# Order of the expert units' buffers, an earlier split of the fourth expert unit, and float32 down units in every other expert

## The reference

```python
logits = jnp.einsum('btd,de->bte', x, router).astype(jnp.float32)
top_v, top_i = lax.top_k(logits, TOP_K)
top_w = jax.nn.softmax(top_v, axis=-1)
...
for e in range(N_EXPERTS):
    out = out + comb[..., e:e + 1] * swiglu(x, w_gu[e], w_dn[e])
```

## Time and profile before

| | us |
|---|---|
| median of 3 runs | 1188.5 |
| lowest, highest | 1188.1, 1192.33 |
| the profiled execution | 1189.18 |
| its span | 1187.5 |
| PE busy | 1131.7 (95% of the span) |
| DVE busy | 948.0 (80%) |
| ACT busy | 715.5 (60%) |
| expert stage, first gate matmul to last down matmul | 748.6 to 1135.4 |
| mean TensorE clock granted | 0.991 of full speed |

### The profile page before, as it was taken

How to read it: one execution, slowest core, us unless ns; L and a number is a source line. 1 busy time by engine, 2 the same in 40 slices (tenths; PEclk the granted TensorE clock), 3 DMA queues, 4 the chain that set the end, 5 groups by cost and what they waited for, 6 DMA issues and landing times.

```text
span 1187.5 us, 31256 instructions
## 1 busy us (share of the span) xinstructions
PE 1131.7 (95%) x13743; PEld 1003.3 (84%) x13743; DVE 948.0 (80%) x1026; ACT 715.5 (60%) x730; POOL 24.9 (2%) x59
## 2 busy tenths in 40 slices
PE   7999999999999999899999998889998999999997
PEld 4788888878888888688888885889998998989976
DVE  5986896777666658996788678689899889898976
ACT  4555644455555445446564435777978669688653
POOL 4000001000000001000000100000000000000000
PEclk8999999999999999999999999899999999999999
DMA  9665566546555654356566564699999999999901
GB/s 268 220 212 178 182 209 215 178 143 205 184 194 195 210 183 142 123 186 207 191 205 202 185 211 153 241 392 393 394 392 393 385 382 394 387 393 390 378 20 38
DMA packets 195673, 289.56 MB, mean 244 GB/s; under 512 B 5208, under 2 KB 132200, under 8 KB 195543
## 3 DMA queue, kind: packets, MB, share of 16 engines
q1 hardware_dynamic: 193830, 283.71, 68.4%
q0 software_dynamic: 1728, 4.16, 1.3%
HBM read 286.53 MB, written 1.52 MB: 243 GB/s over the span
## 4 chain that ended last, share of the span: by engine, by line
PE 82%; DVE 12%; issue 3%; ACT 3%; DMA 0%; SPq 0%; DVEq 0%; ACTq 0%
PE acc L595 16%; PE acc L597 16%; PE acc L596 16%; DVE wl L1361 6%; PE acc L909 4%; PE acc L874 4%; PE acc L877 4%; PE acc L876 4%; PE acc L580 2%; PE acc L581 2%; PE acc L587 2%; PE acc L929 2%; PE acc L926 2%; PE acc L928 2%; PE aux L827 2%
## 5 line engine op out<-in xcount | busy, mean ns | idle before, releaser
L1361 DVE SCALAR_TENSOR_TENSOR wl<-raw,wh 128x2048 f16<-128x2048 f32 x177 | 403.8, 2288 | 116.7 <-ACT wh L1007 116.3
L595 PE MATMUL acc<-xn,wh 128*128 128x264 f16 x1424 | 393.0, 276 | 2.2 <-DVE wl L1361 2.2
L597 PE MATMUL acc<-xn,wl 128*128 128x264 f16 x1424 | 393.0, 276 | 0.0
L596 PE MATMUL acc<-xn,wh 128*128 128x264 f16 x1424 | 393.0, 276 | 0.0
L1007 ACT ACTIVATE wh<-raw 128x2048 f16<-128x2048 f32 x177 | 336.0, 1908 | 1.4 <-PE acc L877 0.6
L874 PE MATMUL acc<-ga,wh 128*128 128x96 f16 x1536 | 204.5, 207 | 10.9 <-issue 5.7
L877 PE MATMUL acc<-ga,wl 128*128 128x96 f16 x1536 | 204.4, 207 | 5.6 <-issue 5.6
L876 PE MATMUL acc<-ga,wh 128*128 128x96 f16 x1536 | 204.3, 207 | 2.1 <-issue 2.1
L874 PEld LDWEIGHTS acc<-ga,wh 128*128 128x128 f16 x1536 | 151.5, 99 | 13.9 <-issue 12.3
L595 PEld LDWEIGHTS acc<-xn,wh 128*128 128x128 f16 x1424 | 139.3, 98 | 23.6 <-ACT wh L1007 2.5
L596 PEld LDWEIGHTS acc<-xn,wh 128*128 128x128 f16 x1424 | 139.3, 98 | 21.0
(11 more groups left out here) (307 smaller groups left out, 1934.1 us busy)
## 6 DMA issues: line engine op xcount, KB each, us to landing
raw<-in_w_in SPq DMA_DIRECT2D x56, 1024.0 KB, 5.1
raw<-in_moe_w_gu SPq DMA_DIRECT2D x42, 1024.0 KB, 13.4
raw<-in_ffn_w_gu SPq DMA_DIRECT2D x24, 1024.0 KB, 5.1
raw<-in_moe_w_dn SPq DMA_DIRECT2D x18, 1024.0 KB, 14.3
raw<-in_ffn_w_dn SPq DMA_DIRECT2D x12, 1024.0 KB, 5.1
ya<-in_moe_w_gu SPq DMA_DIRECT2D x11, 1024.0 KB, 13.6
ot_rows<-in_moe_w_gu SPq DMA_DIRECT2D x10, 1024.0 KB, 13.3
xa<-in_moe_w_gu SPq DMA_DIRECT2D x10, 1024.0 KB, 13.0
```

What stands on the lines that cost most here:

```text
L595: nc.tensor.matmul(bank, hi, x[:, 0, x0 + k, :], start=(k == 0), stop=False)
L596: nc.tensor.matmul(bank, hi, x[:, 1, x0 + k, :], start=False, stop=False)
L597: last = nc.tensor.matmul(bank, lo, x[:, 0, x0 + k, :], start=False, stop=(k == k_chunks - 1))
L1361: op(V.scalar_tensor_tensor(out=wl[:, s, 0:size], in0=raw_slot[raw_turn(n)[0]][:, 0:size], scalar=WS, in1=wh[:, s, 0:size], op0=ALU.mult, ...
```

## The change

Three things are changed. The order of the raw buffers is another: `raw` 2 moves back by two places and `raw` 3 by three, to the last of the ten, and OT, XB, XN, XA and UB come one place earlier each. The fourth expert unit is split in the routing stage: its `hi` stands behind that of the third, its `lo` behind the first one-hot. And only experts 0, 2, 4 and 6 keep direct units: the last two down units of experts 1, 3 and 5 are split like the others. `split_groups` counts the split groups up to q, for the waits.

```diff
-TURN_OF_SLOTS = (YA, 0, 1, 2, OT, XB, 3, XN, XA, UB)
+TURN_OF_SLOTS = (YA, 0, 1, OT, XB, 2, XN, XA, UB, 3)
...
-DIRECT = {dn_unit(e, d) for e in range(NE - 1) for d in range(MOE_DN - 2, MOE_DN)}
+DIRECT = {dn_unit(e, d) for e in range(0, NE, 2) for d in range(MOE_DN - 2, MOE_DN)}
...
-    return q % GROUPS < SPLIT_GROUPS or q // GROUPS == NE - 1
+    return q % GROUPS < SPLIT_GROUPS or q // GROUPS % 2 == 1
+
+
+def split_groups(q):
+
+    return sum(is_split(i) for i in range(q + 1))
...
-                    pe.wait_ge(hid_ready, 2 * FFN_IT + SPLIT_GROUPS * e + d // 2 + 1)
+                    pe.wait_ge(hid_ready, 2 * FFN_IT + split_groups(GROUPS * e + d // 2))
...
             hi(N_MOE + LEAD - 1)
+            hi(N_MOE + LEAD)
             norm_hi()
...
             def gate_or_up(e, u):
                 n, q = gu_unit(e, u), GROUPS * e + u // 4
-                hi(ahead(n))
+                if n > N_MOE:
+                    hi(ahead(n))
...
-                vec_e.wait_ge(hid_hi, q // GROUPS * SPLIT_GROUPS + q % GROUPS + 1)
+                vec_e.wait_ge(hid_hi, split_groups(q))
...
-                lo(ahead(n))
+                if n > N_MOE:
+                    lo(ahead(n))
...
             one_hot(0, sel_ready)
+            lo(N_MOE + LEAD)
             slot_weights(0)
```

More of the change, by code:

```diff
@@ L230, in program @@
         hid_32 = w1_half[:, n_split:4 * EC * CAP].bitcast(F32).rearrange("p (r n) -> p r n", r=2)
-        hid_last = w1_half[:, n_split:4 * EC * CAP].rearrange("p (r s n) -> p r s n", r=2, s=2)[:, (NE - 1) % 2]
+        hid_last = w1_half[:, n_split:4 * EC * CAP].rearrange("p (r s n) -> p r s n", r=2, s=2)[:, 1]
         def hid_half(q, i):
```

## The result

| | median | against before |
|---|---|---|
| before, 7 runs | 1188.65 us (1185.62 to 1192.33) | |
| changed, 7 runs | 1192.14 us (1191.26 to 1194.37) | ratio 1.0031, 95% interval 1.0016 to 1.0045, so +1.9 to +5.3 us |
| profiled execution of changed | 1193.02 us, span 1191.3 | before: 1189.18, span 1187.5 |

A forecast was written before the change was run, and what follows sets the result against it. The prediction took the loop ACT, DVE, PE to bound the expert stage, with DMA just keeping up. Delays of 1.1 + 1.1 + 0.8 = +3.0 us at three turn ends gave 1191.5 us, range 1183.5 to 1196.5.

The forecast's parts named there:

- Bound: Expert stage: bound by the loop ACT, DVE, PE, with PE last; the DMA queue keeps up and no more.
- Buffers and early split: Routing stage and first loads: earlier transfers and early split of the fourth unit, cost 0, gain 0.
- the 8.5 us of head start: Expert loads: four earlier transfers put loading 8.5 us ahead, worth nothing by itself as no engine waits for a transfer.
- The cost of PE beside a busy DMA: PE from 744 to 754 us: gaps of about 1 us could appear beside now busy DMA engines, 0 to +1.
- DVE's lag: Ends of turns 2, 4, 6: extra `lo` work delays the next turn's first down unit, +1.1, +1.1, +0.8 us.
- PE's saving: Turns 2, 4, 6: split units save PE 3.1 us each, 9.4 in all, which do not come out.
- Behind the boundary: After turn 2: PE leads again, DVE's lag shrinks from 1.6 to 0.6 us, under the slack; turns 4 and 5 repeat it.
- The sum: Whole kernel: 1.1 + 1.1 + 0.8 = +3.0 us, so 1191.5; bounds +1 to +5, chance 0.59.
- DMA wall: Rival, expert stage: bytes alone bound it, so loading 8.5 us earlier ends 8.5 us earlier, 1180.0; chance 0.12.
- Shorter gaps: Rival, turns 3 and 5: PE's gaps are fetches queued behind weight packets and halve, 4 us, giving 1187.5; chance 0.11.
- DVE not refilled: Rival, ends of turns 2, 4, 6: DVE still waits for ACT, 3.9 us each, 1200.2, half refilled 1196; chance 0.13.

The follow-up runs named there:

- e_small_loads: Kernel before, each expert unit moved by two transfers of half its size on the same queue: -0.2 us against before (-1.8 to +1.4).
- e_buffers: Changed kernel with the direct units of before, so only the new buffer order and early split: +1.0 us against before (-0.2 to +2.1).
- e_half_after: Changed kernel, only the first half of each expert unit's rows transferred from the 21st unit on, stale values otherwise: +1.1 us against before (-0.5 to +2.6).
- e_units: Changed kernel with the buffers and loads of before, so only the six more split down units: +3.7 us against before (+2.4 to +4.9).
- e_buffers_hold: Kernel before plus new buffer order and early split, transfer into XN held until the first gather ends on PE: -1.8 us against before (-2.7 to -0.7).
- e_half_loads: Kernel before, only the first half of each expert unit's rows transferred from the 21st unit on, stale values otherwise: -11.1 us against before (-12.8 to -9.4).
- e_hold: Changed kernel with the transfer into XN held until the first gather ends on PE: +1.0 us against before (-0.2 to +2.1).

## Why the prediction came out right, step by step

- **Bound.** That no engine waits for a transfer was right for the stretch that was read, 760 to 1060 us. Behind it ACT does, up to 3.2 us at 1107.8, and it costs nothing there; in e_small_loads even some 16 us of such waits cost nothing. Loading stands closer behind the loop than I had it. That PE is last in a loop of three was half of it: the loop alone would run 93.9 us a pair. I had seen the gaps of 1.02 and 0.95 us in the earlier trace rows and took them for a fixed price.
- **Buffers and early split.** Four issues, the DMA rate, the early `hi` and the early `lo` came where they were put, the issue into YA 3.3 us later (4.7 less the 1.4 by which the stage begins later), so the 8.5 us of head start were not reached. The cost of PE beside a busy DMA, "0 to +1", is the mis-sized term: 2.24 us in the first gather, and 3.2 us up to gu 1.0 with the longer low clock. Its counterpart, a pause of 1.87 us and a low clock that leave turn 1, was not in the sum at all; the two together are the +1.0 (-0.2 to +2.1) of e_buffers against a forecast of 0.
- **DVE's lag.** `lo` of dn 2.0 1.6 later: measured 1.56. dn 2.0 1.1 later: measured 1.1, with the releaser named. PE's saving does not come out: right, and e_half_after shows it with nothing else in its way.
- **Behind the boundary.** "Turn 3 runs as before, 1.1 late" failed in both directions. The low clock adds 1.6 us, which no step had; and fetch pauses that turn 3 had before are fewer (from 888 to 930 us PE has 2 gaps over 0.45 us instead of 4). The pair ends 0.7 late instead of 1.1, the next 0.8 instead of 1.1, the last 0.2 instead of 0.8. In the profile the three add up to 1.7 instead of 3.0.
- **The sum.** 1191.5 was forecast and 1192.14 measured. Part of that nearness is luck: +1.7 in the pairs, +0.4 up to gu 2.0 and 0.2 in the last turn make 2.3 us from the first issue to the last down unit, against 0.8 us more or less between executions. In the two profiles another 1.4 us of the difference of 3.8 lie ahead of the first expert unit. The e_units runs, +2.4 to +4.9, hold the +3.0.
- **Rivals.** DMA wall: false for the change, as with half the bytes e_half_after is 2.6 us faster than the changed kernel and its first pair as long; not refuted for the buffers alone, where e_buffers_hold keeps a head start of about 4 us and is 1.8 us faster. (The stage has 144 units, 18 for each of 8 experts, not 148.) Shorter gaps: false as put, since from 830 to 1125 us the DMA engines move 387 GB/s in the changed kernel and 389 before; but its premise was right: lighter traffic takes the pauses away. DVE not refilled: false, DVE has no idle time from 864 to 897 us.

The Trainium skill (Runtime: NRT & Kernel Launch, Instruction fetch mechanics) calls the crossing of an instruction block mostly hidden. e_half_loads agrees, with 45 instruction packets and no pause; the kernel before, with full engines, does not: 44 packets and 24 pauses, 17.5 us. By the Trainium skill (DMA: Bandwidth & Descriptors, Queues, rings and completion order) an engine changes queues between packets, so a fetch would wait for one packet, typically some 9 to 17 descriptors. A packet as the profile counts them takes 0.10 us for weights (102.5% of 16 engines over 295 us, by 48435 packets); whether it is a packet of the page or one of its descriptors no run shows. The wait would be 0.1 us in the first case and, an estimate by the page's figure, 0.9 to 1.7 us in the second. The first gather's fetch began 2.5 us later beside full engines than without, longer than either.

## What to carry to other kernels

Where a profile shows pauses marked issue on a busy engine, set them beside the load on the DMA engines before taking them as given: half the traffic took away 17.5 us of them here. Then ask of every engine how long its loop would be without them, as that is the room that a change on a second engine really has; here the pauses covered 6.6 of the 8.3 us that the six units cost in the three pairs. Read the list of waits to the end of the stage and not over a part of it. And price a new wait of PE of about 2 us with what the clock can take behind it, not by its length alone.

## What the runs showed of the hardware that I had not expected

- Behind a pause or wait of PE of 1.6 to 2.6 us the granted clock fell to some 0.6 over 4 us in ten places of the table, at 1.6 us of PE's work each; waits of 1.2 and 1.3 us had no such stretch behind them. Nor had the wait of 2.3 us at dn 4.0 in e_hold and those of 2.6 us at dn 4.0 and dn 6.0 in e_half_after, so the length alone does not decide.
- An instruction packet of 16 KB takes about 1.1 us whether the DMA engines are full or nearly idle. With full engines PE resumes 2.3 to 2.7 us behind the packet's start where it had to wait for one (all but one of the pauses over 0.45 us in each of the ten profiles with all the bytes).
- One instruction fetch that goes through undisturbed was worth more than loading 4 MB of weights 7 us earlier: the hold took 2.7 us off the changed kernel.
